# The last layer norm of a decoder step, written out by rows of tokens through diagonal products

## What is computed

```
def layer_norm(x, g, b):
    mu = jnp.mean(xf, -1, keepdims=True)
    var = jnp.mean(jnp.square(xf - mu), -1, keepdims=True)
    y = (xf - mu) * lax.rsqrt(var + LN_EPS) * g + b
...
xp = layer_norm(DEEPNORM_ALPHA * xp + 0.5 * swiglu(xp, *f2), ln_g[layer, 2], ln_b[layer, 2])
xs = layer_norm(DEEPNORM_ALPHA * xs + 0.5 * swiglu(xs, *f2), ln_g[layer, 2], ln_b[layer, 2])
```

## Time and profile before

| | |
|---|---|
| median of 3 runs | 2529.04 us (2525.97 to 2529.35) |
| the profiled execution | 2529.85 us |
| its span, first to last instruction | 2528.2 us, 46326 instructions |
| mean granted clock of TensorE | 0.982 of full |
| busy: TensorE, weight loads | 2406.3 us (95%), 2268.4 us (90%) |
| busy: VectorE, ScalarE, GpSimd | 1628.0 (64%), 1086.1 (43%), 458.9 (18%) |
| DMA | 417.31 MB, 165 GB/s mean |

### The profile page before, as it was taken

The page is one execution under the profiler, slowest core; times in us unless marked ns, Lnnn a source line. Parts: engine busy times, 40 slices in busy tenths (PEclk is TensorE's granted clock), DMA queues, the critical chain, the costliest instruction groups (busy, mean ns, idle before and its releaser), DMA issues.

```text
span 2528.2 us, 46326 instructions
## 1 busy us (share of the span) xinstructions
PE 2406.3 (95%) x18811; PEld 2268.4 (90%) x18811; DVE 1628.0 (64%) x2536; ACT 1086.1 (43%) x1663; POOL 458.9 (18%) x532
## 2 busy tenths in 40 slices
PE   7999999999998999999999999999999889999998
PEld 6988998999787777789999999999999889999997
DVE  4787776665764555567686566466656585587555
ACT  3433455433553333443254534554433537354333
POOL 4896800002100111200111101021001000121000
PEclk9999999999999999999899999999999999999999
DMA  8667776445346777644566556555555556555553
GB/s 179 176 177 190 205 198 192 125 117 143 116 136 207 221 239 226 164 123 128 142 175 175 164 148 208 169 153 150 154 149 148 169 165 215 156 158 146 150 150 96
DMA packets 676278, 417.31 MB, mean 165 GB/s; under 512 B 31555, under 2 KB 639683, under 8 KB 676067
## 3 DMA queue, kind: packets, MB, share of 16 engines
q1 hardware_dynamic: 669538, 393.98, 54.1%
q0 software_dynamic: 6528, 20.37, 2.5%
HBM read 395.51 MB, written 18.78 MB: 164 GB/s over the span
## 4 chain that ended last, share of the span: by engine, by line
PE 78%; DVE 12%; issue 3%; ACT 3%; DMA 2%; SPq 2%; POOL 0%; POOLq 0%; ACTq 0%; DVEq 0%
PE ps L256 21%; PE ps L257 20%; PE ps L258 20%; DVE w_lo L251 4%; PE ps L881 2%; PE ps L882 2%; PE ps L883 2%; ACT w_hi L242 2%; PE ps L2280 1%; PE ps L1593 1%; PE ps L1642 1%; DMA w_raw<-in_ffn_w_up 1%; DVE x L531 1%; PE ps L1614 1%; DVE h_lo L435 1%
## 5 line engine op out<-in xcount | busy, mean ns | idle before, releaser
L251 DVE TENSOR_TENSOR w_lo<-w_raw,w_hi 128x1024 fp32r<-128x1024 f32 (+1 forms) x648 | 825.0, 1278 | 623.9 <-ACT w_hi L242 620.9
L256 PE MATMUL ps<-x_hi,w_hi 128*128 128x256 f32 (+1 forms) x3200 | 969.3, 303 | 49.4 <-DVE w_lo L251 35.9
L257 PE MATMUL ps<-x_lo,w_hi 128*128 128x256 f32 (+1 forms) x3200 | 955.9, 299 | 0.0
L258 PE MATMUL ps<-x_hi,w_lo 128*128 128x256 f32 (+1 forms) x3200 | 955.5, 299 | 0.0
L242 ACT ACTIVATE w_hi<-w_raw 128x1024 fp32r<-128x1024 f32 (+1 forms) x648 | 669.6, 1035 | 553.8 <-PE ps L258 399.5
L256 PEld LDWEIGHTS ps<-x_hi,w_hi 128*128 128x128 f32 x3200 | 616.2, 193 | 68.4 <-DVE w_lo L251 53.6
L257 PEld LDWEIGHTS ps<-x_lo,w_hi 128*128 128x128 f32 x3200 | 616.7, 193 | 1.1 <-issue 0.2
L258 PEld LDWEIGHTS ps<-x_hi,w_lo 128*128 128x128 f32 x3200 | 616.1, 193 | 0.0
L256 PE MATMUL ps<-h_hi,w_hi 128*128 128x256 f32 (+1 forms) x1408 | 423.9, 301 | 12.3 <-DVE w_lo L251 9.5
L257 PE MATMUL ps<-h_lo,w_hi 128*128 128x256 f32 (+1 forms) x1408 | 414.5, 294 | 0.0
L258 PE MATMUL ps<-h_hi,w_lo 128*128 128x256 f32 (+1 forms) x1408 | 414.4, 294 | 0.0
(11 more groups left out here) (263 smaller groups left out, 2192.8 us busy)
## 6 DMA issues: line engine op xcount, KB each, us to landing
w_raw<-in_ffn_w_gate SPq DMA_DIRECT2D x176, 512.0 KB, 4.2
w_raw<-in_ffn_w_up SPq DMA_DIRECT2D x176, 512.0 KB, 3.9
w_raw<-in_ffn_w_down SPq DMA_DIRECT2D x128, 512.0 KB, 4.0
w_raw<-in_w_in_ab SPq DMA_DIRECT2D x56, 512.0 KB, 4.0
w_raw<-in_ffn_w_down SPq DMA_DIRECT2D x64, 384.0 KB, 3.5
arena<-in_cache_k SPq DMA_DIRECT2D x64, 256.0 KB, 4.2
arena<-in_cache_v POOLq DMA_DIRECT2D x64, 256.0 KB, 4.8
w_raw<-in_w_out_ab SPq DMA_DIRECT2D x16, 512.0 KB, 3.9
```

What stands on the lines that cost most here:

```text
L251: dve.tensor_tensor(T.w_lo[:, u % RING, 0:n], T.w_raw[:, u % RAW, 0:n], T.w_hi[:, u % RING, 0:n].bitcast(F32), ALU.subtract).then_inc(T.w_ ...
L256: pe.matmul(out, w_hi, m_hi, start=first, stop=False)
L257: pe.matmul(out, w_hi, m_lo, start=False, stop=False)
L258: return pe.matmul(out, w_lo, m_hi, start=False, stop=last)
```

## The change

Group B's last norm becomes a class of its own, `LastNorm`; `alone` goes from `Norm`, everything else is the same.

- The mean is taken off as before (L771 in the changed file). ScalarE squares all eight tiles (L761) into eight places of their own.
- The variance is made by rows of tokens: the squares are the weights, and the moving operand is one column of ones, so that each token's sum lands in its own partition: 3 products for each feature tile, 24 in all (L742), into three columns of bank 2.
- The factor is one value for each partition then: a root of 128x2 and of 64x1 (L763, L764), a reciprocal of the same (L773, L774).
- The centred x goes straight into products (L753): weights x (features by tokens), moving operand a 128x128 diagonal matrix of the gains. That turns and scales it at once, before the factor is known. The six halves have a bank each (4, 5, 6, then 7, 0, 1). The first three halves are made before the variance products, the last three behind them.
- VectorE takes all six out of PSUM with `ps * factor + bias` (L779) into `y_rows`; SP stores each.
- The eight diagonals are made ahead, from `T.ident`, one in each of eight steps of `f3b` on VectorE (L726), and the biases of all features are loaded once to all 128 partitions by SP (L721, 512 KB), behind a wait for the last residual of `OB2`, the output projection ahead of `f3a`'s last part.

```diff
+class LastNorm(Norm):
+    def __init__(self, T, M, g, row, scale, at):
+        super().__init__(T, g, row, scale, False)
+        cut = M.arena.cut
+        self.bias_rows, self.diag, self.sq = cut(at, D_MODEL), cut(at + D_MODEL, KT, P), cut(at + 2 * D_MODEL, KT, g.n)
+        self.by_row, self.var_ps = cut(at + 2 * D_MODEL + KT * g.n, 3), T.ps[:, BANKS[2], 0:len(g.tiles)]
+        self.places = halves(g)
+
+    def bank(self, n):
+        return ((4, 5, 6), (7,) + BANKS[:2])[n // 3][n % 3]
+
+    def load(self, sp, biases):
+        sp.dma_start(self.bias_rows, biases.partition_broadcast(P)).then_inc(self.T.const_loaded.h, 16)
+
+    def diagonals(self, dve):
+        T = self.T
+        for k in range(KT):
+            dve.tensor_scalar(self.diag[:, k, :], T.ident[:, :], T.ln_gain[:, self.row, k:k + 1], None, ALU.mult)\
+               .then_inc(T.const_ready.h, 1)
+            yield
+
+    def tensor(self, pe, moved):
+        T = self.T
+        pe.wait_ge(T.acc_added.h, self.added + KT - 1)
...
+        pe.matmul(self.ps, T.ones[:, :], self.acc, start=True, stop=True).then_inc(T.sum_done.h, 1)
+        pe.wait_ge(T.const_ready.h, 4 + KT)
+        self.to_rows(pe, 0)
+        for k in range(KT):
+            pe.wait_ge(T.squared.h, self.squared + k + 1)
+            for i, t in enumerate(self.g.tiles):
+                m = P if t < PT else NS
+                mm = pe.matmul(self.var_ps[0:m, i:i + 1], self.sq[:, k, i * P:i * P + m], T.ones[:, 0:1],
+                               start=(k == 0 and i == 0), stop=(k == KT - 1), skip_group_check=True)
+        mm.then_inc(T.var_done.h, 1)
+        self.to_rows(pe, 1)
+
+    def to_rows(self, pe, q):
+        T = self.T
+        for k in range(4 * q, 4 * q + 4):
+            pe.wait_ge(T.centred.h, self.centred + k + 1)
+            for n, (t, of, m) in enumerate(self.places):
+                if of == q:
+                    mm = pe.matmul(T.ps[0:m, self.bank(n), (k % 4) * P:(k % 4 + 1) * P], T.x[:, k, t * P:t * P + m],
+                                   self.diag[:, k, :], start=True, stop=True)
+        mm.then_inc(T.y_turned.h, 1)
+
+    def scalar(self, act):
+        T = self.T
+        for k in range(KT):
+            act.wait_ge(T.centred.h, self.centred + k + 1)
+            act.activation(self.sq[:, k, :], self.x(k), ACT.Square).then_inc(T.squared.h, 1)
+        act.wait_ge(T.var_done.h, self.var + 1)
+        act.activation(self.by_row[:, 0:2], self.var_ps[:, 0:2], ACT.Sqrt, bias=self.eps)
+        act.activation(self.by_row[0:NS, 2:3], self.var_ps[0:NS, 2:3], ACT.Sqrt, bias=self.eps[0:NS])\
+           .then_inc(T.rstd_ready.h, 1)
+
+    def vector(self, dve, rows, turned):
...
+        dve.wait_ge(T.rstd_ready.h, self.rooted + 1)
+        T.dve_chain(dve, dve.reciprocal(self.by_row[:, 0:2], self.by_row[:, 0:2]))
+        T.dve_chain(dve, dve.reciprocal(self.by_row[0:NS, 2:3], self.by_row[0:NS, 2:3]))
+        dve.wait_ge(T.const_loaded.h, 2 * 16)
+        for n, (t, q, m) in enumerate(self.places):
+            cols, i = slice(q * 512, (q + 1) * 512), t - self.g.tiles[0]
+            dve.wait_ge(T.y_turned.h, turned + q + 1)
+            dve.scalar_tensor_tensor(rows[0:m, t, cols], T.ps[0:m, self.bank(n), :], self.by_row[0:m, i:i + 1],
+                                     self.bias_rows[0:m, cols], ALU.mult, ALU.add).then_inc(T.y_moved[0].h, 1)
...
@@ sync
             run(out_sync(T, sp, OB2))
+            sp.wait_ge(T.res_done.h, OB2.res + KT)
+            N5B.load(sp, I["ln_b"][DEPTH - 1, 2])
             run(ffn(ffn_sync, sp, f3a[2:]))
...
@@ tensor
-            run(after(N5B.tensor(pe), store_columns(pe, B)))
+            N5B.tensor(pe, (len(A.tiles), len(A.tiles)))
@@ vector
-            weave(ffn(ffn_vector, dve, f3b), after(N5A.vector(dve), store_vector(T, dve, A, y_rows, before[A])))
-            run(after(N5B.vector(dve), store_vector(T, dve, B, y_rows, before[B])))
+            weave(ffn(ffn_vector, dve, f3b), after(after(N5A.vector(dve), store_vector(T, dve, A, y_rows, 0)),
+                                                    N5B.diagonals(dve)))
+            N5B.vector(dve, y_rows, turned_a)
@@ gpsimd
-            run(N5B.gpsimd(pool))
```

More of the change, by code:

```diff
@@ L461, with __init__ @@
     STEPS = 9
-    def __init__(self, T, g, row, scale, products, alone=False, slack=0):
-        self.alone, self.steps, n = alone, self.STEPS + 3 * slack, slack
+    def __init__(self, T, g, row, scale, products, slack=0):
+        self.steps, n = self.STEPS + 3 * slack, slack
         self.square_at, self.var_at, self.root_at = 1 + n, 4 + n, 4 + 2 * n
@@ L477, in __init__ @@
         self.sq_added, self.var, self.rooted, self.normed = (
-            c.take(k) for c, k in ((T.sq_added, KT if alone else KT - 1), (T.var_done, 1), (T.rstd_ready, 2), (T.normed, KT)))
+            c.take(k) for c, k in ((T.sq_added, KT - 1), (T.var_done, 1), (T.rstd_ready, 2), (T.normed, KT)))
         self.affine, self.rounded, self.ready = (
@@ L506, in tensor @@
                 pe.matmul(self.ps, T.ones[:, :], self.acc, start=True, stop=True).then_inc(T.sum_done.h, 1)
[L507 to L512, removed]
+            if i == self.var_at:
                 pe.wait_ge(T.sq_added.h, self.sq_added + KT - 1)
@@ L572, in gpsimd @@
         for i in range(self.steps):
-            if i in (self.square_at, self.square_at + 1) and not self.alone:
+            if i in (self.square_at, self.square_at + 1):
                 for k in self.half(i, self.square_at):
@@ L714, in store_sync, with sync @@
         sp.dma_start(dst[:, q * 512:(q + 1) * 512], rows[0:m, t, q * 512:(q + 1) * 512]).then_inc(T.stored.h, 16)
+class LastNorm(Norm):
[18 more added lines that the diff above has]
+        pe.wait_ge(T.acc_added.h, self.added + KT - 1)
+        for sem, value in zip(T.y_moved, moved):
+            pe.wait_ge(sem.h, value)
+        pe.matmul(self.ps, T.ones[:, :], self.acc, start=True, stop=True).then_inc(T.sum_done.h, 1)
[23 more added lines that the diff above has]
+            act.activation(self.sq[:, k, :], self.x(k), ACT.Square).then_inc(T.squared.h, 1)
+        act.wait_ge(T.var_done.h, self.var + 1)
+        act.activation(self.by_row[:, 0:2], self.var_ps[:, 0:2], ACT.Sqrt, bias=self.eps)
+        act.activation(self.by_row[0:NS, 2:3], self.var_ps[0:NS, 2:3], ACT.Sqrt, bias=self.eps[0:NS])\
+           .then_inc(T.rstd_ready.h, 1)
+    def vector(self, dve, rows, turned):
+        T = self.T
+        dve.wait_ge(T.sum_done.h, self.sums + 1)
+        for k in range(KT):
+            dve.scalar_tensor_tensor(self.x(k), self.ps, -1.0 / D_MODEL, self.x(k), ALU.mult, ALU.add).then_inc(T.centred.h, 1)
+        dve.wait_ge(T.rstd_ready.h, self.rooted + 1)
[7 more added lines that the diff above has]
+                                     self.bias_rows[0:m, cols], ALU.mult, ALU.add).then_inc(T.y_moved[0].h, 1)
+    def sync(self, sp, rows, moved, y_prompt, y_sample):
+        T = self.T
+        for n, (t, q, m) in enumerate(self.places):
+            cols = slice(q * 512, (q + 1) * 512)
+            sp.wait_ge(T.y_moved[0].h, moved + n + 1)
+            dst = y_prompt[t * P:(t + 1) * P, :] if t < PT else y_sample
+            sp.dma_start(dst[:, cols], rows[0:m, t, cols]).then_inc(T.stored.h, 16)
@@ L2771, in layers @@
         F3B = Ffn(B, ffn_3, N4B.ready, N4B.affine + KT)
-        N5B = Norm(T, B, 5, 2.0, False, alone=True)
+        N5B = LastNorm(T, M, B, 5, 2.0, TT * D_MODEL)
         f3b = parts(F3B, (0, 1, 2), N5B)
-        before = {A: 0, B: 2 * len(A.tiles)}
-        whole = {A: N5A.affine + KT, B: N5B.affine + KT}
+        turned_a = 2 * len(A.tiles)
         y_rows = cut(0, TT, D_MODEL)
@@ L2781, in ffn @@
                 yield from of(T, eng, part)
-        def store_columns(pe, g):
-            yield from store_tensor(T, pe, g, before[g], whole[g])
         def norm_and_s5(norm, s5):
@@ L2840, in _ @@
             y_prompt, y_sample = (O[n] for n in ("y_prompt", "y_sample"))
-            for g in (A, B):
-                store_sync(T, sp, g, y_rows, before[g], y_prompt, y_sample)
+            store_sync(T, sp, A, y_rows, 0, y_prompt, y_sample)
+            N5B.sync(sp, y_rows, len(A.tiles), y_prompt, y_sample)
             sp.wait_ge(S.stored.h, 6 * 16)
@@ L2889, in _ @@
             weave(ffn(ffn_scalar, act, f3a[2:]), N4B.scalar(act))
-            weave(ffn(ffn_scalar, act, f3b), after(N5A.scalar(act), store_scalar(T, act, A, y_rows, before[A])))
-            run(after(N5B.scalar(act), store_scalar(T, act, B, y_rows, before[B])))
+            weave(ffn(ffn_scalar, act, f3b), after(N5A.scalar(act), store_scalar(T, act, A, y_rows, 0)))
+            N5B.scalar(act)
         @block.vector
```

11 lines of the change are left out of this document (3 added, 8 removed).

## The result

| | before | after |
|---|---|---|
| median | 2528.76 us (11 runs, 2525.97 to 2532.67) | 2534.0 us (11 runs, 2531.4 to 2539.98) |
| the profiled execution, its span | 2529.85, 2528.2 | 2533.63, 2532.0 |
| from the sum over features (L506, now L735) to the end of the span | 23.1 us | 26.0 us |
| mean granted clock of TensorE | 0.982 | 0.982 |

The ratio after to before is 1.0024, with a 95% interval of 1.0016 to 1.0031: slower by 4 to 8 us. The forecast was 2525.6 with a range to 2532.3, so it was wrong. Two of its signs of being wrong came too: a clock of 0.50 at the second group of L753, and over 6.5 us for L742.

A forecast was written before the change was run, and what follows sets the result against it. The prediction took the end as a single file of dependent work; repriced, the span ends at 2524.8 instead of 2528.2, -3.4 us. That put the profiled execution at 2526.4 and the median, 0.8 lower, at 2525.6, range 2522.5 to 2532.3.

The forecast's parts named there:

- (a): First half of the diagonal products on TensorE: 24 instructions at half clock, 5.1 us.
- (b): Variance by rows on TensorE: 48 one-column instructions, clock rising to full early in them, ending at 2516.7.
- (c): Second half of the diagonal products on TensorE: 2.65 us at full clock plus 0.27 to drain.
- rival 3: Variance: a weight load hides behind nothing before a one-column product; 13.6 us there, +7.6 us, time 2536.6; chance 0.05.
- Rival 2: Variance: one-column products don't keep the clock up; time 2531.9 or 2528.7; chance 0.25.
- point of decision: Where Rival 2 starts to decide: the tail's 96 TensorE instructions taking 16.2 us instead of 12.9, 0.17 each.
- The branch in which the clock rises in the diagonals and falls in the variance: Part of Rival 2: about half of (b) and all of (c) slow; -0.3 us, time 2528.7; chance 0.13.
- Half clock at the start: First diagonal products: TensorE at 1.2 GHz as before at that moment, 0.213 us per instruction, full clock at 2512.9.
- Rival 1: Tail's products: full clock comes earlier, at 2509.5; -5.0 us, time 2524.0; chance 0.20.
- Rival 4: Variance: weight loads cost the same at both clock levels, (b) 4.5 us flat; time 2524.9; chance 0.06.
- Rival 5: Ahead of the tail: the broadcast or the diagonals delay TensorE by up to 2.7 us; time 2528.3; chance 0.07.

The follow-up runs named there:

- ahead: The kernel before plus only the broadcast of the biases and the eight diagonals, unused by anything; ratio to before 1.0001, tail 20.6 us.
- full: The changed kernel with the sample tile's products taking the last 128 tokens as weights, so the weight column count never changes; ratio to before 1.0000, tail 20.7 us.
- wide: The changed kernel with 128 columns of ones instead of one as the variance's moving operand; ratio to before 1.0026, tail 22.5 us.
- grouped: The changed kernel with the sample tile's products placed behind those of the two full tiles in each piece; ratio to before 0.9998, tail 20.2 us.
- before_b: The kernel before, unedited, executed once more for a second trace; profiled 2526.08 us, tail 20.6 us.
- acc: The changed kernel with the squares added up on VectorE, three one-column products left, and all diagonal products first; ratio to before 0.9989, tail 18.0 us.
- varlast: The changed kernel with the variance products moved behind all diagonal products; one execution, profiled 2534.22 us, tail 26.0 us.
- widefull: The changed kernel with both 128 columns of ones in the variance and 128-column weights for the sample tile; ratio to before 0.9993, tail 17.9 us.
- wide32: The changed kernel with 32 columns of ones instead of one as the variance's moving operand; one execution, profiled 2536.47 us, tail 26.6 us.

## Why the prediction was wrong

The structure was right. The three pieces of TensorE follow one another without a gap, the roots and reciprocals take 0.26 + 0.24 + 0.17 + 0.15 us, less than half of the reciprocal alone before, the first three moves hide behind the products, the last three take 2.06 us (1.9 forecast), and from the last move to the end of the span it is 2.8 us (3.3). The broadcast and the diagonals cost nothing, as ahead shows. What failed are the sizes of (a), (b) and (c), and the number from which they were subtracted:

| term | forecast | measured | clock's part | column changes' part |
|---|---|---|---|---|
| (a) first diagonal half | 5.1 | 4.06 | -2.4 | +1.2 |
| (b) variance | 5.1 | 8.48 | +1.8 | +1.5 |
| (c) second diagonal half | 2.9 | 7.10 | +3.1 | +1.1 |

The parts of (a) are from full (2.92 at full clock with no change of count): 5.1 - 2.7 by clock, 4.06 - 2.92 by changes. Those of (c) are from wide (7.10 - 4.03) and full (4.03 - 2.92). For (b), a feature tile with no change of count is 0.56 us at full clock, as forecast and about what the loads of after give piece by piece (four at 0.11, two at 0.055); the real one is 0.742, so 8 x 0.18 = 1.5 by changes, and 8.48 - 8 x 0.742 = 2.5 by clock, of which the forecast had 0.7. In sum about 3.8 us by column changes and 2.5 by clock. These parts are worked out from single traces; how much each kernel gained in the timed runs stands in the table of ratios.

1. **The pace in (a), (b) and (c) was added up from rows of unmixed products.** The step took L1294 and L2226, each a run of one shape, as 4 x 0.11 + 2 x 0.058 for a sequence that alternates. For products sorted by width these paces hold (grouped). Sixteen changes of column count in the diagonal products cost 0.14 to 0.17 us each at full clock and 0.25 at half, and sixteen in the variance about 0.1 each. No rival had this; rival 3, a load that hides behind nothing, had the mechanism but for every load, and the measured loads of equal width do hide. The 24 transposes of L686 could not have warned of it. They change the column count only three times (eight of 128, four of 64, eight, four), and even there their loads start 0.213 us apart as everywhere else at half clock (before_b).
2. **The clock was read as a matter of when, not of what runs.** Rival 2 (0.25 in all) named the mechanism, and wide, acc and varlast confirm it: it falls in the one-column products, and in after it isn't back at full before the last product; in full and grouped it is. Its point of decision, 0.17 us for one of 96 instructions, held: after needs 19.6 / 96 = 0.20, and is slower. The branch in which the clock rises in the diagonals and falls in the variance comes nearest to what happened (the clock didn't have to rise, it was full from the start); it was priced at 2528.7 since the column changes and the lower baseline of point 3 were missing from it. The evidence against it, a full clock at 64 columns "beside dense work", was weaker than it was taken for.
3. **Half clock at the start was carried over from one trace of before.** It is one of two ways in which before itself runs. Against the tail of 23.1 us the change loses 2.9, against the 20.6 it loses 5.4. The four traces of this end split two and two; the ratios tell which is usual, if the tails of the other traces are typical: full (20.7 us) would be 0.9990 against 23.1 and 1.0000 against 20.6, and is 1.0000 (from 0.9991); after would be 1.0011 or 1.0021, and is at least 1.0016. The interval of widefull too excludes the 23.1, by which it would be 0.9979. The sum comes out: 2525.6 forecast, 6.3 for the longer tail (26.0 against the 19.7 forecast), 2.5 for the baseline, less 0.3 since the median of before over 11 runs is lower than over 3, makes 2534.1.

Rival 1 was half right in its premise (full clock from the start) and wrong in its gain. Rival 4 falls: a weight load of 128 columns in L742 lasts 0.19 us at full clock and 0.33 at half, and the starts of loads lie 0.11 and 0.21 us apart. The Trainium skill, "TensorE: Matmul & The Clock Gate", section "LDWEIGHTS (loading the stationary operand)", gives one formula for a load, its columns divided by 1.2 in nanoseconds, and parts no levels of the clock. This trace does not bear that out: the distance of 0.11 us at full clock is near its 107 ns, the one at half is twice that. Rival 5 falls with ahead.

What stays open. Why the timed runs of wide show a ratio of 1.0026, when its profiled tail is only 1.9 us above the usual one of before, which would be 1.0008. The profiled execution is the fastest of its twelve. Two others took 2545 us at a mean clock of 0.977 and 0.978; the remaining ten read 0.982 or more, so what lengthens most of them doesn't show in the clock. Why L686's transposes don't pay for a changed column count: they are one instruction each where a product of L753 is two, but no run tested whether that is why. And why before's clock falls before L510 in some executions.

## What to carry to other kernels

fp32 products that alternate between two widths of weights can lose the early weight load at each change; sort them by width, or make the narrow ones as wide as the others even if half of the result is thrown away. Products of one moving column were no faster here than those of 128 when all weights had one width (0.112 us an instruction for both), and they can take TensorE's clock down for what follows; a sum over partitions of many tiles is better added up on an idle VectorE first, with one narrow product behind it. Price a mixed sequence from a mixed row, and look at a short tail in more than one trace before a few microseconds of it are taken as the baseline.

## What the runs showed of the hardware

- fp32 products that alternate between 128 and 64 columns of weights, 128 columns moving: 1.00 us for a feature tile at full clock against 0.67 without alternation, 1.77 against 1.28 at half. Both directions cost. The same products sorted by width take 3.04 us for 24 (grouped), against 4.06.
- A feature tile of three products with weights of the same shapes is faster with one moving column than with 128 when the widths alternate (0.74 against 1.00 us at full clock): in the single records of the trace the first 64-column load starts 0.21 us behind the load before it, with 128 moving columns 0.31.
- TensorE's granted clock went from 1.00 to 0.50 within back-to-back products of 1 column (after, full, grouped, varlast) or 32 (wide32) with new weights for each, 1.7 to 3.3 us into them, and stayed at 1.00 through 8.03 us of products of 128 (wide). The profile has the engine busy all the time in both.
- Before's own end runs in two ways that differ by 2.5 us, 7.5 or 4.6 us for the eight products of L510, with the same instructions.
